# The passage from up to down units in a fast-matrix MLP: split order, who squares the last unit, and where its four sums are made

## The chip, the core and the metric

The kernel runs on one NeuronCore of one Trainium2 chip. Its engines work side by side: TensorE (PE) multiplies into PSUM banks, VectorE (DVE), ScalarE (ACT) and GpSimd (POOL) work elementwise, and SyncE (SP) issues the DMA transfers. Each engine takes its own instructions in the order in which they are written; they meet only at semaphores. The metric is device time in microseconds (us), median of three runs.

## The reference, cut to what matters

A decoder trunk of two layers (a hybrid mixer, then a sparse-attention mixer), 1024 tokens by 1024 channels in fp32. Each layer ends in the same MLP, which is all that the change touches:

```
def squared_relu_mlp(u, w1, w2):
    return jnp.square(jax.nn.relu(u @ w1)) @ w2
...
        h = h + squared_relu_mlp(rms_norm(h, norm_mlp[layer]), mlp_w1[layer], mlp_w2[layer])
```

## The kernel before, in words

Every fp32 operand is split into a high part (rounded by ACT) and a low part (operand minus high part, by DVE or POOL), and each product is three matmuls: high by high, low by high, high by low. One such matmul of 128x512 starts every 0.23 us when PE is not held up.

**The units.** The MLP of each layer runs 14 "up" units (`fast_up`, the hidden columns) and then 14 "down" units (`fast_down`, d = 0 to 13), each a 2x2 block multiplication by Strassen's scheme in Winograd's form: 7 products (i = 0 to 6) of block sums in place of 8, each product 12 matmuls. The weights' sums are made by POOL (`unit_sums`) and split by ACT and DVE (`unit_high`, `unit_low`), unit by unit, ahead of PE.

**The hidden side.** After an up unit, DVE forms the hidden blocks (add a bank of PSUM to a block set aside by ACT in CX, CW, CY, then relu and square) and four sums of them (`hidden_sums`), and SP stores all seven to `hid_d` in HBM (`store_hidden`). The down units take hidden sub-blocks q = 0 to 13 as their other operand, split into high and low by `sub_high` (ACT) and `sub_low` (DVE; POOL for three of q = 1). Down units d and d+1 use the pair q = d and q = d+1 (d even). q = 0 and 1 come straight from SBUF (up units 11 and 12); the others are reloaded from `hid_d` (`load_sub`). The last up unit, 13, is q = 13, used only from d = 12 on. Its blocks are written into `HO[1]` (tiles HOA1, HOB1) over those of unit 11 (q = 0), so each square has to wait until its block of q = 0 is split.

**The passage.** Around the end of up unit 13, DVE runs a list written out by hand: `last_out` (adds that free the PSUM banks), `last_square`, the splits of q = 0 and 1 (`sub_low(q, i)`), those of the weights of unit 14, the first down unit (`unit_low(N_UP, i)`), the first `collect` (adding a down product from PSUM to H) and the four sums of unit 13. `fast_down(0)` on PE waits for its splits by a count in the order in which DVE makes them.

**What SP does then.** In one queue: `load_unit(16)` into the buffer of unit 14's weights, free when unit 14's last splits are done; `store_hidden(13)`; `load_sub(3)`; when the store has landed, the reload of half of the residual H from `hm_d` (it lies where HOA1 and HOB1 were). DVE's `collect(1, 0)`, the first of down unit 1, waits for this reload; PE's product 2 of down unit 1 waits for `collect(1, 0)`, since it goes into the same bank. In the same way product 4 of each down unit waits for `collect(d, 2)`.

Of the kernel before, what the change touches and what calls it, by code (L numbers as in the profile page):

```python
# [85 lines left out]
def build_program(nc, xT, pieces, cst, sel, prm, gatew, relx, onehot, w1c, w2c, blkind, out):  # L86
    ctx = ExitStack()
    with ctx:
# [250 lines left out]
        q_lo = Again(m_rs, 1)  # L339
        q_lop = sem("hidden_lo_pool")  # L340
        s_spill = Again(x_in[1], 16)
        f_back = Again(x_in[2], 16)
# [44 lines left out]
        def sub_raw(q, i):  # L387
# [7 lines left out]
            return (U_rawh, U_raw)[(i - 1) // 3][:, 5 + (i - 1) % 3, T1]  # L395

        def sub_no(L, q, i):

            return 95 * L + 7 * q + i + 1 - 3 * (q > 1)

# [259 lines left out]
        def mlp_pe(pe, first_units, mm3, piece_read, pieces_read_now, sum_squares, spread, p0, layer):  # L660
# [44 lines left out]
            def fast_up(u):  # L705

                gu = N_UP * layer + u
                for i in range(7):
                    b = U_BANKS[u % 2][PROD_BANK[i]]
                    pe.wait_ge(*unit_ready(layer, u, i))  # L710
                    if u == 0 and i in (1, 2, 4, 5):
                        pe.wait_ge(*s_slo.at(4 * layer + (1, 2, 0, 3, 4)[i - 1]))
                    if u == 1 and i == 0:
                        pe.wait_ge(up_free, 8 * layer + 12)
                    if i == 0 and u >= 2:
                        pe.wait_ge(*f_relu.at(gu - 1))
                    elif i == 1 and u >= 2:
                        pe.wait_ge(*f_hid.at(10 * (gu - 2) + 5))
                    elif i == 2:
                        pe.wait_ge(*f_copy.at(3 * gu + 1))  # L720
                    elif i == 3 and u >= 2:
                        pe.wait_ge(*f_hid.at(10 * (gu - 2) + 1))
                    elif i == 4:
                        pe.wait_ge(*f_copy.at(3 * gu + 3))
                    elif i == 6:
                        pe.wait_ge(*f_hid.at(10 * gu + (3 if u < 13 else 2)))
                    for k in range(4):
                        w = slice(k * P, (k + 1) * P)
                        last = mm3(ps[:, b, :], RH[i][:, w], RL[i][:, w], U_SIDE[i][0][:, k, :], U_SIDE[i][1][:, k, :],
                                   k == 0 and i in (0, 1, 3), k == 3, i not in (0, 1, 3))  # L730
                    last.then_inc(f_up.sem, 1)

            def fast_down(d):

                gd, n = N_DOWN * layer + d, N_UP + d
                for i in range(7):
                    pe.wait_ge(*unit_ready(layer, n, i))
                    if d % 2 == 0:
                        pe.wait_ge(*q_lo.at(sub_no(layer, d + 1, min(i, 6 if d else 3))))
                    if d == 0 and i > 3:  # L740
                        pe.wait_ge(*sub_late(layer, i))
                    if d == 0 and i == 0:
                        pe.wait_ge(*f_hid.at(10 * (14 * layer + 13) + 4))
                    if d == 1 and i == 0:
# [36 lines left out]
        def mlp_act(act, layer):  # L781
# [47 lines left out]
            def hidden_last(u):  # L829
# [6 lines left out]
                act.wait_ge(*f_relu.at(gu + 1))  # L836
                A(H21[:], H21[:], ACT.Square).then_inc(sq21.sem, 1)

            def sub_high(q, i):
# [5 lines left out]
                else:  # L845
                    act.wait_ge(*q_in[q % 2].at(16 * (2 + q % 2) * (6 * L + q // 2)))
                act.wait_ge(*sub_free(L, q, i))
                A(sub_tile(q % 3, i)[0], sub_raw(q, i), ACT.Copy).then_inc(q_hi.sem, 1)

# [18 lines left out]
            for u in range(N_UP):  # L868
                for i in range(7):
# [10 lines left out]
                    if u == N_UP - 1 and i >= 3:  # L880
                        if i == 3:
                            sub_high(0, 6)
                        for x in ((0, 1), (2, 3), (4, 5), ())[i - 3]:
                            sub_high(1, x)
            for d in range(N_DOWN - 1):
                for i in range(7):
# [11 lines left out]
        def mlp_dve(dve, sum_first, norm_steps, layer):  # L898
# [43 lines left out]
            def last_out(j):  # L942
# [4 lines left out]
                c = (CX, CW, CY)[j][:]  # L947
                V_.tensor_tensor(c, ps[:, U_BANKS[1][(1, 0, 2)[j]], :], c, ALU.add).then_inc(f_hid.sem, 1)

            def last_square(j):  # L950

                gu = N_UP * L + 13
                c = (CX, CW, CY)[j][:]
                dve.wait_ge(*q_lo.at(sub_no(L, 0, (0, 6, 3)[j])))
                dve.wait_ge(*f_hid.at(10 * gu + (1, 2, 4)[j]))
                V_.scalar_tensor_tensor(HO[1][(0, 6, 3)[j]], c, 0.0, c, ALU.max, ALU.mult).then_inc(f_hid.sem, 1)

            def hidden_sums(u):
# [9 lines left out]
                dve.wait_ge(*f_hid.at(10 * gu + 9))  # L968
                V_.tensor_tensor(t[5], t[3], t[2], ALU.subtract).then_inc(f_hid.sem, 1)

            def sub_low(q, i):
# [78 lines left out]
            last_out(1)  # L1050
            last_square(0)
            sub_low(0, 5)
            last_out(2)
            sub_low(0, 6)
            last_square(1)
            unit_low(N_UP, 3)
            sub_low(1, 0)
            last_square(2)
            for i in range(1, 4):
                sub_low(1, i)  # L1060
            unit_low(N_UP, 4)
            dve.wait_ge(*q_lo.at(sub_no(L, 1, 3)))
            collect(0, 0)
            hidden_sums(N_UP - 1)
            dve.wait_ge(q_lop, 3 * (L + 1))
            for d in range(N_DOWN):
                for i in range(7):
# [6 lines left out]
                    if i and d + 2 < N_DOWN:  # L1074
                        sub_low(d + 2, i - 1)
                    if d == N_DOWN - 1 and i in (4, 5):
                        hidden(0, 2 * (i - 4))
# [80 lines left out]
        def mlp_sp(sp, load, layer):  # L1158
# [33 lines left out]
            def store_hidden(u):  # L1192

                sp.wait_ge(*f_hid.at(10 * (14 * L + u) + 10))
                dma(hid_d[u][:, 0:4, :], HOA[u % 2][:]).then_inc(f_out[u % 2].sem, 16)
# [2550 lines left out]
```

## Time and profile before

| what | value |
|---|---|
| time, median of 3 runs | 2550.36 us (2550.3 to 2551.29) |
| the profiled execution, its own time | 2550.74 us |
| its span, first to last instruction | 2548.8 us |
| PE busy | 2485.8 us (98%) |
| DVE, POOL, ACT busy | 1773.0, 1208.6, 1108.6 us |
| mean granted clock of PE | 0.994 of full speed |

How to read it: the two MLPs are the long dense stretches of PE. The passage of layer 0 lies at about 817 to 857 us of the span, that of layer 1 at 2221 to 2261 us; up to the end of up unit 13, layer 1 repeats layer 0 some 1403.77 us later. Times in the rows below are microseconds from the span's start.

### The profile page before, as it was taken

The page shows a single profiled execution, that of the slowest core. Times are in us where ns is not written, and L with a number is a line of the kernel's source. Part 1 is how long each engine was busy: PE and PEld are TensorE (multiplying, and loading weights), DVE is VectorE, ACT ScalarE, POOL GpSimd, SP SyncE. Part 2 cuts the span into 40 slices and gives each one's busy share as a digit, 9 for nine tenths or more (in the row PEclk, how much of TensorE's full clock was granted, in tenths as well). Part 3 has the DMA queues.
Part 4 walks back from the last instruction along what each step waited for, and adds up shares of the span by engine and source line. Part 5 has one row for each costly group of instructions (what it writes and reads, how often), then busy time and mean ns, then how long its engine had stood idle before and what let it go on. Part 6 is the DMA issues. An engine that isn't in the chain of part 4 may idle for free.

```text
span 2548.8 us, 38266 instructions
## 1 busy us (share of the span) xinstructions
PE 2485.8 (98%) x14136; PEld 2009.7 (79%) x14136; DVE 1773.0 (70%) x2859; ACT 1108.6 (43%) x2142; POOL 1208.6 (47%) x939
## 2 busy tenths in 40 slices
PE   8999999999999999999999999999999999999999
PEld 5778667888887888887877777788788888778887
DVE  6554755476777999973037877676646777899994
ACT  4526644243334344322136666566524333434431
POOL 5462677234445454434215777546523444544441
PEclk9999999999999999999999999999999999999999
DMA  4110003223443544412321112353222344354441
GB/s 173 34 50 34 1 2 116 79 87 138 158 159 108 216 174 143 145 44 122 103 82 57 55 55 76 90 150 88 112 83 87 137 153 165 107 215 155 164 145 66
DMA packets 91711, 275.78 MB, mean 108 GB/s; under 512 B 9879, under 2 KB 39191, under 8 KB 76871
## 3 DMA queue, kind: packets, MB, share of 16 engines
q1 hardware_dynamic: 87976, 255.18, 29.4%
q10 hardware_dynamic: 3552, 18.18, 1.8%
q8 instruction: 114, 1.87, 0.3%
q14 instruction: 69, 0.57, 0.1%
HBM read 197.50 MB, written 73.86 MB: 106 GB/s over the span
## 4 chain that ended last, share of the span: by engine, by line
PE 90%; DVE 3%; issue 2%; POOL 2%; ACT 1%; DMA 1%; DVEq 0%; ACTq 0%; POOLq 0%
PE ps L1738 23%; PE ps L1743 22%; PE ps L1742 22%; PE ps L2305 5%; PE ps L2321 5%; PE ps L2280 2%; PE ps L2295 1%; POOL MX L1537 1%; PE ps L2296 1%; PE ps L1967 1%; PE ps L1996 1%; PE ps L1981 1%; PE ps L2229 1%; PE ps L2121 1%; PE ps L1860 0%
## 5 line engine op out<-in xcount | busy, mean ns | idle before, releaser
L1738 PE MATMUL ps<-U_hi,RH 128*128 128x512 f32 x912 | 356.8, 391 | 10.1 <-issue 10.1
L1742 PE MATMUL ps<-U_lo,RH 128*128 128x512 f32 x912 | 356.7, 391 | 0.0
L1743 PE MATMUL ps<-U_hi,RL 128*128 128x512 f32 x912 | 356.5, 391 | 0.0
L1136 POOL TENSOR_TENSOR RL<-RAW,RH 128x512 fp32r<-128x512 f32 x112 | 152.7, 1363 | 380.6 <-ACT RH L819 380.6
L819 ACT ACTIVATE RH<-RAW 128x512 fp32r<-128x512 f32 x280 | 175.3, 628 | 285.1 <-PE ps L1743 278.9
L1738 PE MATMUL ps<-U_hi,W_hi 128*128 128x512 f32 (+2 forms) x656 | 261.7, 399 | 11.9 <-DVE U_lo L3015 10.5
L1743 PE MATMUL ps<-U_hi,W_lo 128*128 128x512 f32 (+2 forms) x656 | 258.1, 393 | 0.0
L1742 PE MATMUL ps<-U_lo,W_hi 128*128 128x512 f32 (+2 forms) x656 | 258.0, 393 | 0.0
L1738 PE MATMUL ps<-SH,RH 128*128 128x512 f32 x656 | 255.5, 389 | 0.9 <-ACT CX L827 0.9
L1743 PE MATMUL ps<-SH,RL 128*128 128x512 f32 x656 | 255.2, 389 | 0.0
L1742 PE MATMUL ps<-SL,RH 128*128 128x512 f32 x656 | 255.2, 389 | 0.0
L1738 PEld LDWEIGHTS ps<-U_hi,RH 128*128 128x128 f32 x912 | 172.3, 189 | 47.0 <-issue 10.9
L927 DVE TENSOR_TENSOR RL<-RAW,RH 128x512 fp32r<-128x512 f32 x168 | 137.0, 816 | 100.3 <-ACT RH L819 100.3
L1743 PEld LDWEIGHTS ps<-U_hi,RL 128*128 128x128 f32 x912 | 172.3, 189 | 36.2
L1742 PEld LDWEIGHTS ps<-U_lo,RH 128*128 128x128 f32 x912 | 172.2, 189 | 35.7
L1121 POOL TENSOR_TENSOR RT<-RAW 128x512 f32<-128x512 f32 x56 | 77.0, 1375 | 234.2 <-PE ps L1743 160.7
L1454 POOL CAST W_hi<-W_raw 128x2048 fp32r<-128x2048 f32 x28 | 58.8, 2100 | 249.0 <-DMA W_raw<-in_pieces 207.7
L819 ACT ACTIVATE RH<-RT 128x512 fp32r<-128x512 f32 x112 | 70.9, 633 | 213.5 <-POOL RT L1126 111.6
L1738 PEld LDWEIGHTS ps<-U_hi,W_hi 128*128 128x128 f32 (+2 forms) x656 | 122.5, 187 | 44.0 <-DVE U_lo L3015 10.9
L1600 POOL TENSOR_SCALAR PX<-PX,rinv,GATE 128x896 f32<-128x896 f32 (+7 forms) x128 | 104.8, 830 | 99.3 <-DVE rinv L3510 99.1
L3518 DVE COPY PT<-ps 128x512 f32<-128x512 f32 (+1 forms) x192 | 94.3, 519 | 82.2 <-PE ps L2305 82.0
L994 DVE TENSOR_TENSOR H<-H,ps 128x512 f32<-128x512 f32 x212 | 136.2, 677 | 20.5 <-PE ps L1743 18.7
(409 smaller groups left out, 6082.2 us busy)
## 6 DMA issues: line engine op xcount, KB each, us to landing
W_raw<-in_pieces SPq DMA_DIRECT2D x30, 1024.0 KB, 5.1
RAW<-in_pieces SPq DMA_DIRECT2D x28, 1024.0 KB, 5.0
RAW<-in_pieces SPq DMA_DIRECT2D x56, 512.0 KB, 8.2
hid_d<-HOA SPq DMA_DIRECT2D x24, 1024.0 KB, 3.9
hid_d<-HOB SPq DMA_DIRECT2D x24, 768.0 KB, 5.4
RHA<-hid_d SPq DMA_DIRECT2D x12, 1024.0 KB, 5.2
RHB<-hid_d SPq DMA_DIRECT2D x12, 768.0 KB, 7.5
U_rawh<-hid_d SPq DMA_DIRECT2D x12, 768.0 KB, 4.8
```

The costliest lines, as they stand in the source:

```text
L819: A(ring(RH[i], n), src, ACT.Copy).then_inc(u_hi.sem, 1)
L927: V_.tensor_tensor(ring(RL[i], n), src, ring(RH[i], n).bitcast(F32), ALU.subtract).then_inc(u_lod.sem, 1)
L994: V_.tensor_tensor(o, o, ps[:, b[m], :], ALU.add).then_inc(f_ev.sem, 1)
L1121: G_.tensor_tensor(ring(RT[1], n), R[B12], R[B11], ALU.subtract).then_inc(u_add.sem, 1)
L1136: G_.tensor_tensor(ring(RL[i], n), quarter(n, (B22, B11)[i - 5]), ring(RH[i], n).bitcast(F32), ALU.subtract).then_inc(u_lop.sem, 1)
L1600: nc.gpsimd.tensor_scalar(p, p, rinv[:, c:c + 1], GATE[:, i, hd * 3 + 1 + br:hd * 3 + 2 + br], ALU.mult, ALU.mult).then_inc(x_nm, 1)
L1738: m = mm(o, a_hi, b_hi, start=first, stop=False, skip_group_check=again)
L1742: mm(o, a_hi, b_lo, start=False, stop=False, skip_group_check=again)
L1743: return mm(o, a_lo, b_hi, start=False, stop=last, skip_group_check=again)
L2305: m = nc.tensor.transpose(ps[:, b, kb % 4 * P:kb % 4 * P + P], prob(U)[0][:, kb * P:(kb + 1) * P], ident)
L2321: m = mm(ps[DK * e:DK * (e + 1), b, x * P:x * P + P], KV[:, k0 + kb, 1 if br == SEL else 3, hd // HPG, :], PT[(2 * s + e) % 4][:, kb * P:( ...
L3518: V_.tensor_copy(PT[U % 4][:, k0 * P:k1 * P], ps[:, rot("p", U, j), 0:(k1 - k0) * P]).then_inc(x_cpv, 1)
```

## The change

- DVE splits q = 0 and q = 1 in the order in which PE's first down unit uses them (`Q_FIRST` gives the place of each in the count), and makes the first `collect` earlier.
- The last unit's relu and square go from DVE (one instruction for each of three blocks) to ACT (a relu and a square for each), after the last weights' split of unit 14. A semaphore of their own (`last_unit_banks_read`) now tells PE that the banks are free. The fourth block's square is written straight into `HO[1][1]`.
- The four sums of unit 13 are not made in the passage. `store_hidden(13)` goes out when the squares are done; the sums are made when q = 13 is back in SBUF, by DVE in down unit 11 (`late_sum`), and ACT's `sub_high(13, i)` of those four blocks waits for them.

```diff
+        Q_FIRST = ((0, 0), (0, 1), (0, 2), (0, 3), (0, 4), (1, 0), (1, 1), (1, 2), (0, 6), (1, 3), (0, 5))
...
                     if d % 2 == 0:
-                        pe.wait_ge(*q_lo.at(sub_no(layer, d + 1, min(i, 6 if d else 3))))
+                        pe.wait_ge(*q_lo.at(sub_no(layer, d + 1, i) if d else
+                                            max(sub_no(layer, 0, i), sub_no(layer, 1, min(i, 3)))))
...
                     if d == 0 and i == 0:
-                        pe.wait_ge(*f_hid.at(10 * (14 * layer + 13) + 4))
+                        pe.wait_ge(last_read, 3 * layer + 3)
...
+            def last_square(n, j):
+                gu = N_UP * L + 13
+                c = (CX, CW, CY)[j][:]
+                act.wait_ge(last_read, 3 * L + j + 1)
+                A(c, c, ACT.Relu).then_inc(f_hid.sem, 1)
+                act.wait_ge(*f_hid.at(10 * gu + 2 * n + 1))
+                act.wait_ge(*q_lo.at(sub_no(L, 0, (0, 6, 3)[j])))
+                A(HO[1][(0, 6, 3)[j]], c, ACT.Square).then_inc(f_hid.sem, 1)
...
+            def late_sum(j):
+                g0 = 10 * (14 * L + 13) + 6
+                r = [sub_raw(13, i) for i in range(7)]
+                if j:
+                    dve.wait_ge(*f_hid.at(g0 + j))
+                else:
+                    dve.wait_ge(*q_in[1].at(48 * (6 * L + 6)))
+                o, x, y, op = ((r[4], r[0], r[1], ALU.subtract), (r[1], r[1], r[6], ALU.add),
+                               (r[2], r[1], r[0], ALU.subtract), (r[5], r[3], r[2], ALU.subtract))[j]
+                V_.tensor_tensor(o, x, y, op).then_inc(f_hid.sem, 1)
...
             last_out(1)
-            last_square(0)
+            sub_low(1, 0)
+            sub_low(1, 1)
+            last_out(2)
+            sub_low(1, 2)
+            sub_low(0, 6)
+            unit_low(N_UP, 3)
+            dve.wait_ge(*q_lo.at(sub_no(L, 1, 2)))
+            collect(0, 0)
+            sub_low(1, 3)
             sub_low(0, 5)
-            last_out(2)
-            sub_low(0, 6)
-            last_square(1)
-            unit_low(N_UP, 3)
-            sub_low(1, 0)
-            last_square(2)
-            for i in range(1, 4):
-                sub_low(1, i)
             unit_low(N_UP, 4)
-            dve.wait_ge(*q_lo.at(sub_no(L, 1, 3)))
-            collect(0, 0)
-            hidden_sums(N_UP - 1)
+            dve.wait_ge(*q_lo.at(95 * L + 11))
...
+                    if d == 11 and i < 3:
+                        for j in ((0, 1), (2,), (3,))[i]:
+                            late_sum(j)
...
             def store_hidden(u):
-                sp.wait_ge(*f_hid.at(10 * (14 * L + u) + 10))
+                if u == N_UP - 1:
+                    sp.wait_ge(*f_hid.at(10 * (14 * L + u) + 6))
+                    sp.wait_ge(*sq21.at(14 * L + u + 1))
+                else:
+                    sp.wait_ge(*f_hid.at(10 * (14 * L + u) + 10))
```

The order of the built programs shows the moves. First DVE in the passage of layer 0, before, from the second `last_out` (CW) to the last split of unit 14's weights (RL4). HOA0 and HOB0 hold q = 1, HOA1 and HOB1 hold q = 0 and then unit 13; `SCALAR_TENSOR_TENSOR` is a `last_square`; U_lo, SL0 and SL1 are the low parts of hidden blocks.

```order
L948 TENSOR_TENSOR CW_130<-ps,CW_130 128x512
L956 SCALAR_TENSOR_TENSOR HOA1_126<-CX_129 128x512
L975 TENSOR_TENSOR SL1_123<-HOB1_128,SH1_120 128x512
L948 TENSOR_TENSOR CY_131<-ps,CY_131 128x512
L975 TENSOR_TENSOR U_lo_88<-HOB1_128,U_hi_87 128x512
L956 SCALAR_TENSOR_TENSOR HOB1_128<-CW_130 128x512
L927 TENSOR_TENSOR RL3_104<-RAW0_115,RH3_97 128x512
L975 TENSOR_TENSOR U_lo_88<-HOA0_125,U_hi_87 128x512
L956 SCALAR_TENSOR_TENSOR HOA1_126<-CY_131 128x512
L975 TENSOR_TENSOR U_lo_88<-HOA0_125,U_hi_87 128x512
L975 TENSOR_TENSOR SL0_122<-HOA0_125,SH0_119 128x512 x2
L927 TENSOR_TENSOR RL4_105<-RAW0_115,RH4_98 128x512
```

The same place with the change:

```order
L972 TENSOR_TENSOR CW_130<-ps,CW_130 128x512
L1003 TENSOR_TENSOR U_lo_88<-HOA0_125,U_hi_87 128x512 x2
L972 TENSOR_TENSOR CY_131<-ps,CY_131 128x512
L1003 TENSOR_TENSOR SL0_122<-HOA0_125,SH0_119 128x512
L1003 TENSOR_TENSOR U_lo_88<-HOB1_128,U_hi_87 128x512
L951 TENSOR_TENSOR RL3_104<-RAW0_115,RH3_97 128x512
L1020 COPY H_70<-ps 128x512 x2
L1003 TENSOR_TENSOR SL0_122<-HOA0_125,SH0_119 128x512
L1003 TENSOR_TENSOR SL1_123<-HOB1_128,SH1_120 128x512
L951 TENSOR_TENSOR RL4_105<-RAW0_115,RH4_98 128x512
L1020 COPY H_70<-ps 128x512 x2
```

The first split of q = 1 (`U_lo<-HOA0`), eighth in the first list, is now second, right behind `last_out` of CW; the three squares are gone; two copies of `collect(0, 0)` stand ahead of the last three splits instead of behind them; the four sums that came behind the copies before are gone too.

Second, DVE at the start of down unit 11 in layer 0, with the change. `U_raw`, `U_rawh` and `RHC` hold q = 13 as reloaded; lines L997 are the four late sums, L1022 and L1033 are `collect`, and the second pair of L1022 with the third is `collect(11, 1)` and `collect(11, 2)`.

```order
L1022 TENSOR_TENSOR H_70<-H_70,ps 128x512 x2
L997 TENSOR_TENSOR U_raw_150<-RHC_149,U_rawh_151 128x512
L997 TENSOR_TENSOR U_rawh_151<-U_rawh_151,U_raw_150 128x512
L1022 TENSOR_TENSOR H_70<-H_70,ps 128x512 x2
L951 TENSOR_TENSOR RL0_101<-RAW0_115,RH0_94 128x512
L1003 TENSOR_TENSOR U_lo_88<-RHC_149,U_hi_87 128x512
L997 TENSOR_TENSOR U_rawh_151<-U_rawh_151,RHC_149 128x512
L1022 TENSOR_TENSOR H_70<-H_70,ps 128x512 x2
L951 TENSOR_TENSOR RL1_102<-RT1_109,RH1_95 128x512
L1003 TENSOR_TENSOR U_lo_88<-U_rawh_151,U_hi_87 128x512
L997 TENSOR_TENSOR U_raw_150<-U_rawh_151 128x512
```

Without the four lines L997 this is the list of before; three of them stand ahead of `collect(11, 2)`.

Third, ACT at the end of the passage, with the change, from the square of the fourth block to the first weights' split of down unit 1 (RH0 from RAW1):

```order
L847 ACTIVATE HOA1_126<-H21_132 128x512
L827 ACTIVATE RH6_100<-RAW0_115 128x512
L854 ACTIVATE CX_129<-CX_129 128x512
L857 ACTIVATE HOA1_126<-CX_129 128x512
L854 ACTIVATE CY_131<-CY_131 128x512
L857 ACTIVATE HOA1_126<-CY_131 128x512
L854 ACTIVATE CW_130<-CW_130 128x512
L857 ACTIVATE HOB1_128<-CW_130 128x512
L827 ACTIVATE RH0_94<-RAW1_116 128x512
```

The six instructions L854 and L857 are new; before, RH0 followed RH6.

## Rows read from the trace of the kernel before

**Rows 1.** PE's waits: engine, line, awaited: us in total, times, longest.
```profile
PE ps L1738 <- issue: 10.1, 2, 5.1
...
PE ps L1996 <- DVE MIX L3266: 4.7, 4, 2.7
...
PE ps L1738 <- DVE U_lo L2912: 2.3, 1, 2.3
```

**Rows 2.** Timeline of PE, layer 0: start, us, line, instruction [idle before].
```profile
828.35 0.54 PE L1738 MATMUL ps<-U_hi,RH 128*128 128x512 f32 x1 [5.05 <-issue]
...
832.07 0.39 PE L1738 MATMUL ps<-U_hi,RH 128*128 128x512 f32 x1
...
854.56 0.39 PE L1738 MATMUL ps<-SH,RH 128*128 128x512 f32 x1
```

**Rows 3.** Timeline of PE, layer 1.
```profile
2232.12 0.77 PE L1738 MATMUL ps<-U_hi,RH 128*128 128x512 f32 x1 [5.05 <-issue]
...
2238.50 0.40 PE L1738 MATMUL ps<-U_hi,RH 128*128 128x512 f32 x1
...
2259.68 0.47 PE L1738 MATMUL ps<-SH,RH 128*128 128x512 f32 x1
```

**Rows 4.** Timeline of DVE in the passage, layer 0.
```profile
826.51 1.75 DVE L975 TENSOR_TENSOR U_lo<-HOA,U_hi 128x512 fp32r<-128x512 f32 x1
...
831.66 0.68 DVE L927 TENSOR_TENSOR RL<-RAW,RH 128x512 fp32r<-128x512 f32 x1
```

**Rows 5.** Timeline of POOL in the passage, layer 0.
```profile
821.39 1.30 POOL L1136 TENSOR_TENSOR RL<-RAW,RH 128x512 fp32r<-128x512 f32 x1 [4.60 <-ACT RH L819]
...
835.80 1.52 POOL L1121 TENSOR_TENSOR RT<-RAW 128x512 f32<-128x512 f32 x1 [6.42 <-PE ps L1743]
```

**Rows 6.** Timeline of ACT, layer 0: the first weights' split of down unit 1.
```profile
833.02 0.63 ACT L819 ACTIVATE RH<-RAW 128x512 fp32r<-128x512 f32 x1 [7.91 <-PE ps L1743]
```

**Rows 7.** Timeline of SP's DMA queue, layers 0 and 1.
```profile
832.37 1.23 SPq L1185 DMA_DIRECT2D RAW<-in_pieces  x2
836.21 0.33 SPq L1195 DMA_DIRECT2D hid_d<-HOA  x1
...
842.93 0.81 SPq L1249 DMA_DIRECT2D H<-hm_d  x2
...
2236.14 1.23 SPq L1185 DMA_DIRECT2D RAW<-in_pieces  x2
2240.87 0.33 SPq L1195 DMA_DIRECT2D hid_d<-HOA  x1
```

**Rows 8.** H reload, layer 0: time from issue to landing of its two transfers.
```profile
DMA to landing us min/median/max: 7.2/8.2/9.3
```

**Rows 9.** Timeline of DVE: `collect(1, 0)` in layer 0 and in layer 1.
```profile
852.64 1.28 DVE L994 TENSOR_TENSOR H<-H,ps 128x512 f32<-128x512 f32 x2
...
2258.84 1.28 DVE L994 TENSOR_TENSOR H<-H,ps 128x512 f32<-128x512 f32 x2 [1.21 <-DMA H<-hm_d]
```

**Rows 10.** Stretches: length, busy (instructions) of five engines, clock, DMA share, GB/s.
```profile
834.00:842.00 8.00, 8.00 (x37) 6.64 (x36) 7.96 (x12) 2.46 (x6) 5.96 (x4) 1.00 1.02 352
...
842.50:852.50 10.00, 10.00 (x45) 8.23 (x44) 10.00 (x14) 4.43 (x9) 3.16 (x3) 1.00 1.03 412
...
2240.60:2241.90 1.30, 1.30 (x7) 1.08 (x6) 1.30 (x3) 0.00 (x0) 0.75 (x1) 1.00 0.56 199
```

**Rows 11.** The same columns: PE's clock after two of its waits.
```profile
1170.00:1173.20 3.20, 3.20 (x8) 2.53 (x9) 3.13 (x5) 1.26 (x2) 0.00 (x0) 0.50 0.00 0
294.40:297.60 3.20, 2.64 (x25) 1.95 (x26) 1.92 (x8) 0.88 (x4) 1.82 (x2) 1.00 0.00 0
```

**Rows 12.** Timeline of DVE and PE in down unit 11, layer 0.
```profile
1045.16 0.69 DVE L994 TENSOR_TENSOR H<-H,ps 128x512 f32<-128x512 f32 x1 [0.43 <-PE ps L1743]
...
1048.73 1.27 DVE L994 TENSOR_TENSOR H<-H,ps 128x512 f32<-128x512 f32 x2
...
1050.40 0.39 PE L1738 MATMUL ps<-SH,RH 128*128 128x512 f32 x1
```

More of the change, by code:

```diff
@@ L340, in build_program @@
         q_lop = sem("hidden_lo_pool")
+        last_read = sem("last_unit_banks_read")
         s_spill = Again(x_in[1], 16)
@@ L395, in sub_raw @@
             return (U_rawh, U_raw)[(i - 1) // 3][:, 5 + (i - 1) % 3, T1]
+        Q_FIRST = ((0, 0), (0, 1), (0, 2), (0, 3), (0, 4), (1, 0), (1, 1), (1, 2), (0, 6), (1, 3), (0, 5))
         def sub_no(L, q, i):
+            if q < 2:
+                return 95 * L + Q_FIRST.index((q, i)) + 1
             return 95 * L + 7 * q + i + 1 - 3 * (q > 1)
@@ L724, in fast_up @@
                         pe.wait_ge(*f_copy.at(3 * gu + 3))
+                    elif i == 6 and u < 13:
+                        pe.wait_ge(*f_hid.at(10 * gu + 3))
                     elif i == 6:
-                        pe.wait_ge(*f_hid.at(10 * gu + (3 if u < 13 else 2)))
+                        pe.wait_ge(last_read, 3 * layer + 2)
                     for k in range(4):
@@ L836, in hidden_last @@
                 act.wait_ge(*f_relu.at(gu + 1))
-                A(H21[:], H21[:], ACT.Square).then_inc(sq21.sem, 1)
+                if u == N_UP - 1:
+                    act.wait_ge(*q_lo.at(sub_no(L, 0, 1)))
+                A(HO[1][1] if u == N_UP - 1 else H21[:], H21[:], ACT.Square).then_inc(sq21.sem, 1)
+            def last_square(n, j):
[6 more added lines that the diff above has]
+                A(HO[1][(0, 6, 3)[j]], c, ACT.Square).then_inc(f_hid.sem, 1)
             def sub_high(q, i):
@@ L847, in sub_high @@
                 act.wait_ge(*sub_free(L, q, i))
+                if q == 13 and i in (1, 2, 4, 5):
+                    act.wait_ge(*f_hid.at(10 * (14 * L + 13) + {1: 8, 2: 9, 4: 7, 5: 10}[i]))
                 A(sub_tile(q % 3, i)[0], sub_raw(q, i), ACT.Copy).then_inc(q_hi.sem, 1)
@@ L884, in mlp_act @@
                             sub_high(1, x)
+            for n, j in enumerate((0, 2, 1)):
+                last_square(n, j)
             for d in range(N_DOWN - 1):
@@ L947, in last_out @@
                 c = (CX, CW, CY)[j][:]
[L948 to L956, printed above, removed]
+                V_.tensor_tensor(c, ps[:, U_BANKS[1][(1, 0, 2)[j]], :], c, ALU.add).then_inc(last_read, 1)
             def hidden_sums(u):
@@ L1192, in store_hidden @@
             def store_hidden(u):
-                sp.wait_ge(*f_hid.at(10 * (14 * L + u) + 10))
+                if u == N_UP - 1:
+                    sp.wait_ge(*f_hid.at(10 * (14 * L + u) + 6))
+                    sp.wait_ge(*sq21.at(14 * L + u + 1))
+                else:
+                    sp.wait_ge(*f_hid.at(10 * (14 * L + u) + 10))
                 dma(hid_d[u][:, 0:4, :], HOA[u % 2][:]).then_inc(f_out[u % 2].sem, 16)
```

## The prediction

> **What bounds the kernel now.** I read PE's waits first. PE hardly waits, and of the few stalls two are of one kind: twice, 5.05 us, on L1738 [rows 1]. The view names no releaser ("issue"), so I took PE's timeline: the stall lies between the last matmul of up unit 13 and the first of down unit 0, in both layers [rows 2, 3]. In the code, PE's count of splits for product 0 includes the first split of q = 1, which DVE makes last but three; in layer 0 that is the instruction of 826.51, which ends at 828.26, just before PE starts. The passage is therefore bound by DVE, and DVE by GpSimd: where a split meets a POOL instruction it takes 1.75 us, where it does not, 0.68 [rows 4], and POOL's own takes 1.30 [rows 5].
>
> The stall costs more than its length. The matmul before it ended at 828.35 - 5.05 = 823.30; matmuls last 0.39 and follow each other at 0.23, so the next could have started at 823.14. After the stall, nine starts take 832.07 - 828.35 = 3.72 us, PE being at the lower of its two clock levels; 99 more bring product 2 of down unit 1 at 854.56, 0.227 each [rows 2]. Without stall and slow clock that product, 108 matmuls in, would start at 823.14 + 24.53 = 847.7: **6.9 us** lost. In layer 1 the same points are 2226.91 and 2251.4, against 2259.68, with fifteen slow starts in 6.38 us [rows 3]: **8.2 us** lost. So 15.1 us, 0.59% of the time, is all that the passage can give.
>
> Then I asked what is late next, so SP's queue and the DMA stretches. DVE's first `collect` of down unit 1 waits for the reload of H. In layer 0 the second reload transfer lands 9.3 us after its issue at about 843.3 [rows 7, 8], at 852.6, and DVE starts at 852.64; in layer 1 DVE sits idle 1.21 us for it, until 2258.84, and PE's product 2 comes at 2259.68, just behind [rows 9, 3]. This reload is already as late as PE can bear.
>
> **The change part by part.**
>
> *The new order of splits.* Until the second `last_out` nothing moves. The two splits that PE now needs follow it without POOL in the way and end near 820.9, the third `last_out` near 821.5: both ahead of 823.14. Product 0 starts without a stall, and the clock has no reason to fall: 6.9 and 8.2 us are won here, if nothing takes them back. For product 2 PE needs `collect(0, 0)` by 828.6. DVE makes three instructions that meet POOL (3 x 1.7 from 821.5), then the two copies (from PSUM; such copies are not slowed), done at 827.8. That fits.
>
> *Squares on ACT.* Six instructions of 0.6 us, 3.6 us. They fall into ACT's idle time of 7.91 us before 833.02 [rows 6]; ACT reaches the next weights' split at about 828.7 instead of 826, and DVE comes to that operand only near 833. Price nothing; with the cover gone, at most 2.7 us.
>
> *DVE after the copies.* PE is now ahead, so POOL's sums for the next unit start at 829, when product 1 ends, and not at 835.8 [rows 5]. The last three splits meet them. Without POOL they would end at 829.6, all three behind a POOL instruction at 832.9; I take 831.8, since one POOL instruction is left of the old unit and one or two of the new fall in. Before it was 832.3 [rows 4]. So `load_unit(16)` is issued only 0.5 us earlier, at 831.9. Next come two copies, a split, and a split of q = 2 behind POOL: `collect(0, 2)` has its first copy at 835.8. PE wants it for product 4 at 834.05: a **new wait of 1.9 us**. It is not an extra term, since a later wait swallows it.
>
> *The H reload.* The store of unit 13 now follows `load_unit(16)` by 1.25 us instead of 3.8 and 4.7 us [rows 7]. But that load, the store, `load_sub(3)` and H go through one set of DMA engines, busy all the while: share 1.02 and 1.03 on both sides of 842.25 [rows 10]. If only bytes count, H lands earlier by the 0.5 us of the load, at 852.1; in layer 1 also by the free 0.44 of 1.3 us [rows 10], 0.6, at 2257.7. That is one bound. The other: the 2.9 MB of load and store, 352 GB/s, would move at the 412 of the stretch behind them, 7.0 us in place of 8.2; with the 0.5, H lands at 850.9 and, with the gap, at 2256.5. I take the middle, 851.5 and 2257.1. The copy takes 0.68 and PE follows within 0.15, so product 2 of down unit 1 starts at 852.35 and 2257.95. Gain: **2.2 and 1.7 us** of the 15.1 (bounds 2.7 to 5.1 together).
>
> *The clock.* PE would reach that product at 847.7 + 1.9 = 849.6, and waits 2.8 us; in layer 1 at 2253.3, and waits 4.6. After 2.3 us (L2912) the clock is at the low level for all of the next 3.2 us; after 2.7 us, at another place (MIX), it is not [rows 1, 11]. I take a fall, since matmuls of this form follow here as behind the first of these, and the smaller of the two prices seen, 3.72 - 9 x 0.227 = 1.7 us; in layer 1 before, it was 6.38 - 15 x 0.227 = 3.0. Cost: **1.7 per layer**, 3.4 (0 to 6.0).
>
> *The late sums.* Four DVE instructions of at least 0.60 each move from the passage, where they held up the store alone, into down unit 11. There DVE is booked out: one pause of 0.43 us at the start of the unit [rows 12]. Three of the four stand ahead of `collect(11, 2)`, whose first copy ends at 1049.4; PE takes it at 1050.40, a margin of 0.9 with the semaphore. Least price: 4 x 0.60 - 0.43 = 2.0 us of lateness, of which the margin may hide 0.9, or all, if no later collect is tight. Highest: each of the three behind a POOL instruction, 3 x 1.75 - 0.9 = 4.4. I take **2.0 per layer**: 1.1 at product 4, the rest when the backlog of the fourth reaches the next unit. Total 4.0 (0 to 8.8).
>
> The Trainium skill's page "SBUF — State Buffer", section "Who interferes with whom", says that a VectorE instruction with two SBUF inputs and a GpSimd one that reads SBUF take a shared port in turn, and the loser is blocked for the whole of the other; one with at most one SBUF input does not contend. The rows agree on which ones meet; on the price they show 1.75 - 0.68 = 1.1 us for a loser, where the page's whole instruction would be the 1.30 of POOL's row. By the page the highest price would be 3 x (0.60 + 1.30) - 0.9 = 4.8 us per layer instead of 4.4. It speaks against the move: the sums have two SBUF inputs.
>
> *Sum.* -3.9 + 3.4 + 4.0 = +3.5 us. The profiled execution took 2550.74 us, 1.94 of them outside its span; with the change 2554.2. The median of the runs is 0.38 below that execution, so **2553.9 us**: +0.14%. A measurement of this kernel tells 0.2%, 5.1 us, from no change.
>
> **The rivals.**
> 1. *The main case*: passage won, given back at the H reload, by the clock and in unit 11. 2551 to 2557. Chance 0.45.
> 2. *The sums are hidden, or the clock stays up.* For it: PE waits nowhere in the down units before, and one 2.7 us wait left the clock alone. -3.9 with one of the two prices gone gives +0.1 or -0.5, with both gone 2546.5. From 2546 to 2551. Chance 0.17.
> 3. *The reload is not the limit.* If transfers queued close together move faster than these stretches show, and H lands before PE arrives (849.6 less 0.8, so by 848.8, 16.9 us after the load's issue where it was 20.2), the 15.1 us are won less the new waits at product 4 (2 x 1.9) and the sums (4.0): -7.3, 2543. Against it: the full DMA share. Chance 0.10.
> 4. *Slower beyond measurement*: the waits in unit 11 reach 2 us, so the clock falls there too (1.7 per layer), and in layer 1 it stays low as long as before (3.0 instead of 1.7): 3.5 + 3.4 + 1.3 = +8.2, 2558.6. It decides at a wait of some 2 us ahead of product 4: two of the three sums behind a POOL instruction. Chance 0.28.
>
> **How the numbers follow.** The prediction is the likeliest case. Faster by over 0.2% is rival 3 alone, 0.10. Slower by over 0.2% is rival 4, and 0.02 from the upper end of the main case: 0.30. The same: the rest, 0.60. The range leaves out rival 3 and the far end of rival 4, about 0.18: 2546 to 2559.
>
> **What would show it.** Right: no PE wait at the start of down unit 0; one of 1 to 2 us ahead of product 4 of down unit 0; one of 2 to 5 us ahead of product 2 of down unit 1, released by L1022 behind a DMA wait on H; 0.50 clock behind it; `load_unit(16)` within 0.7 us of before, though its store comes 2.6 us earlier; waits of about 1 us in down units 11 and 12. Wrong: H landing before 850, which makes it faster; no waits in units 11 and 12, which takes 4 us off; a wait at product 0 or 2 of down unit 0, which would mean that the order of splits did not remove the stall.

## The result, and the profile after

| what | before | after |
|---|---|---|
| time, median | 2551.47 us (2550.3 to 2553.48, 9 runs) | 2557.74 us (2552.76 to 2563.42, 9 runs) |
| ratio to before, with its interval | | 1.0021 (1.0012 to 1.003) |
| the profiled execution, its own time | 2550.74 us | 2557.03 us |
| its span; mean clock of PE | 2548.8 us; 0.994 | 2555.2 us; 0.992 |

The change makes the kernel 0.21% slower, 5.4 us by the ratio. The stall ahead of down unit 0 [rows 1] is gone; two other waits have come in the passage, and a short one in down unit 11. PE's timeline in the profile after, layer 0 and then layer 1; the bracket is the idle time before the instruction and what ended it:

```profile
825.35 0.39 PE L1771 MATMUL ps<-U_hi,RH 128*128 128x512 f32 x1
...
838.29 0.47 PE L1771 MATMUL ps<-SH,RH 128*128 128x512 f32 x1 [1.90 <-DVE H L1020]
...
856.91 0.77 PE L1771 MATMUL ps<-SH,RH 128*128 128x512 f32 x1 [4.73 <-DVE H L1022]
...
861.28 0.40 PE L1775 MATMUL ps<-SL,RH 128*128 128x512 f32 x1
...
1055.88 0.47 PE L1771 MATMUL ps<-SH,RH 128*128 128x512 f32 x1 [0.85 <-DVE H L1022]
...
2231.38 0.39 PE L1771 MATMUL ps<-U_hi,RH 128*128 128x512 f32 x1
...
2262.83 0.76 PE L1771 MATMUL ps<-SH,RH 128*128 128x512 f32 x1 [4.62 <-DVE H L1022]
...
2267.59 0.40 PE L1776 MATMUL ps<-SH,RL 128*128 128x512 f32 x1
```

825.35 and 2231.38 are product 0 of down unit 0, without a wait. The kernel before could have started it at 823.14 and 2226.91, so the after trace runs 2.21 us late into the passage of layer 0 and 4.47 into that of layer 1. I take these off when I compare: the 4.47 holds what layer 0 lost, but most of the 2.21 arose in the first 60 us, which the change does not touch.

The other rows are the ends of three waits: product 4 of down unit 0 (838.29), product 2 of down unit 1 (856.91, 2262.83), product 4 of down unit 11 (1055.88). Product 2 of down unit 1 comes at 856.91 - 2.21 = 854.70, against 854.56 before [rows 2]: in layer 0 nothing is left of the passage's gain. In layer 1 it comes at 2258.36, against 2259.68 [rows 3]: 1.3 us are left. Behind it the clock is low until 861.28 and 2267.59.

SP's queue of the profile after, layer 0, answers to [rows 7]:

```profile
834.09 1.23 SPq L1214 DMA_DIRECT2D RAW<-in_pieces  x2
835.42 0.56 SPq L1228 DMA_DIRECT2D hid_d<-HOA  x1
...
844.88 0.81 SPq L1282 DMA_DIRECT2D H<-hm_d  x2
```

The store follows the load by 1.33 us, where it was 3.84. Yet the reload behind it is issued at 844.88 - 2.21 = 842.67, against 842.93. DVE's `collect(1, 0)`, to [rows 9], shows when it landed:

```profile
856.08 2.48 DVE L1022 TENSOR_TENSOR H<-H,ps 128x512 f32<-128x512 f32 x4 [6.09 <-DMA H<-hm_d]
...
2261.99 2.48 DVE L1022 TENSOR_TENSOR H<-H,ps 128x512 f32<-128x512 f32 x4 [5.98 <-DMA H<-hm_d]
```

On before's time that is 853.87 and 2257.52. Before, the reload landed near 852.6 and at 2258.84: in layer 0 it is 1.2 us later, not earlier, though it is issued a little sooner. From issue to landing its two transfers take (to [rows 8]):

```profile
DMA to landing us min/median/max: 8.6/9.7/10.8
```

The DMA's stretches come next (length, busy and instructions of five engines, clock, DMA share, GB/s; to [rows 10]). The changed kernel:

```profile
835.50:839.00 3.50, 1.60 (x7) 1.04 (x7) 3.50 (x5) 1.97 (x4) 3.10 (x2) 1.00 0.90 259
...
845.00:852.00 7.00, 7.00 (x32) 5.62 (x30) 4.99 (x6) 2.52 (x5) 2.42 (x2) 1.00 1.05 415
...
834.09:854.09 20.00, 16.18 (x71) 12.75 (x69) 15.90 (x21) 7.89 (x15) 8.71 (x7) 1.00 0.93 354
```

and before:

```profile
834.00:835.80 1.80, 1.80 (x10) 1.49 (x9) 1.76 (x4) 0.17 (x1) 0.00 (x0) 1.00 0.96 312
...
841.00:842.50 1.50, 1.50 (x8) 1.25 (x7) 1.50 (x2) 1.50 (x4) 1.50 (x1) 1.00 0.86 210
...
832.37:852.37 20.00, 20.00 (x90) 16.48 (x89) 19.94 (x27) 8.24 (x15) 9.62 (x6) 1.00 0.94 350
```

While `load_unit(16)` and the store run side by side, the DMA engines are busy (0.90) and move 259 GB/s, against 415 behind. The Trainium skill's "HBM Reference", section "Specifications (TRN2)", says that a core streaming alone measures about 425 GB/s: the stretch behind agrees, the one of load and store does not. But this is not what makes the reload late. The kernel before has slow stretches too, 312 GB/s while the load runs alone and 210 near the store's end, and over the 20 us from the load's issue the engines move no fewer bytes with the change (354 GB/s) than before (350).

What is late is the reload's tail, its last packets. The reload moves 256 packets of 8 KB. By the trace's records of single packets the 240th starts 19.1 us after the load's issue in layer 0 of both kernels, the last one at 19.5 us before and at 21.2 with the change. In layer 1 before has such a tail as well (20.2 and 21.9 us; 19.2 and 21.1 with the change). Of these four places only layer 0 of before was spared it. Why the tail is long in one place and short in another, no run here shows.

### The profile page after: what moved, and what is told of

It is laid out like the page before. It is cut to its first block, busy times and chain, and to the rows that moved or that the text cites. A ratio compares the mean times of both kernels' runs of the same rounds, so it can differ in the third digit from the quotient of the medians.

```text
span 2555.2 us, 38274 instructions
## 1 busy us (share of the span) xinstructions
PE 2487.1 (97%) x14136; PEld 2009.3 (79%) x14136; DVE 1766.3 (69%) x2853; ACT 1115.7 (44%) x2154; POOL 1206.4 (47%) x939
## 4 chain that ended last, share of the span: by engine, by line
PE 86%; DVE 6%; issue 2%; DMA 2%; POOL 2%; ACT 1%; SPq 0%; DVEq 0%; ACTq 0%; POOLq 0%
PE ps L1771 21%; PE ps L1776 21%; PE ps L1775 21%; PE ps L2338 5%; PE ps L2354 5%; PE ps L2313 2%; PE ps L2328 1%; PE ps L2329 1%; POOL MX L1570 1%; PE ps L2000 1%; PE ps L2029 1%; PE ps L2014 1%; DVE SL L1003 1%; DMA H<-hm_d 1%; DMA hid_d<-HOB 1%
## 5 line engine op out<-in xcount | busy, mean ns | idle before, releaser
L1022 DVE TENSOR_TENSOR H<-H,ps 128x512 f32<-128x512 f32 x212 | 136.3, 677 | 33.4 <-PE ps L1776 20.6
L1771 PEld LDWEIGHTS ps<-SH,RH 128*128 128x128 f32 x656 | 124.2, 189 | 44.5 <-issue 18.9
```

What stands on the lines that cost most here:

```text
L1022: V_.tensor_tensor(o, o, ps[:, b[m], :], ALU.add).then_inc(f_ev.sem, 1)
L1771: m = mm(o, a_hi, b_hi, start=first, stop=False, skip_group_check=again)
```

## The experiments

All were timed against the kernel before on the same chip, so ratios are compared, not medians. A ratio's interval is about 0.1% either way, 2.5 us; the traces decide between neighbours. Waits are those of layer 0.

| run | median us | ratio (interval) | PE's waits: unit 0 / unit 1 / units 11 and 12 |
|---|---|---|---|
| changed kernel | 2557.74 | 1.0021 (1.0012 to 1.003) | 1.90 / 4.73 / 0.85 |
| e1, reload ahead of load_sub(3) | 2551.78 | 0.9998 (0.9989 to 1.0006) | 1.90 / 2.94 / 0.85 |
| e2, store ahead of load_unit(16) | 2545.56 | 0.9973 (0.9964 to 0.9981) | 1.91 / 0 / 0.84 |
| e3, both | 2546.22 | 0.9973 (0.9963 to 0.9983) | 1.91 / 0 / 0.84 |
| b1, e1's move in the kernel before | 2552.92 | 1.0 (0.9991 to 1.0008) | 5.06 (ahead of it) / 0 / 0 |
| e4, evictions first in unit 0 | 2556.72 | 1.0017 (1.0008 to 1.0026) | 1.29 / 5.24 / 0.85 |
| e5, e3 and splits behind the evictions | 2542.83 | 0.9958 (0.9945 to 0.9971) | 0 / 0 / 0.85 |
| e6, sums back in the passage | 2556.66 | 1.0013 (1.0005 to 1.0022) | 5.66 / 0 / 0 |
| e9, e6 with squares on DVE | 2558.41 | 1.0018 (1.0009 to 1.0027) | 7.78 / 0 / 0 |
| e7, e3 with sums one step later | 2548.29 | 0.9977 (0.9968 to 0.9987) | 1.91 / 0 / 0.74, 0.58 |
| e10, e5 with sums on POOL | 2543.26 | 0.9958 (0.9944 to 0.9971) | 0 / 0 / 0.87, 0.61 |
| e11, e5 without the sums | 2536.87 | 0.9935 (0.9921 to 0.9948) | 0 / 0 / 0 |
| e12, e5 with sums in the passage | 2552.21 | 1.0 (0.999 to 1.0011) | 4.46 / 0 / 0 |

### Is the reload the limit, and what makes it late?

My theory: the passage's gain is lost to the reload, which queues behind other transfers. Rival: squares and late sums cost the time. e1:

```diff
             store_hidden(13)
-            load_sub(3)
             sp.wait_ge(*stored(L, 13))
             for c in (2, 6):
                 dma(H[:, c:c + 2, :], hm_d[:, c:c + 2, :]).then_inc(f_back.sem, 16)
+            load_sub(3)
             load_residual(0)
```

> The reload of H is issued ahead of the three transfers of load_sub(3); nothing else changes. Theory (the end of the passage is set by the landing of the reload, which queues behind load_unit(16), the store and load_sub(3) in the same DMA engines): without the 1.75 MB of load_sub(3) beside it the store lands 1 to 2 us earlier and the reload is alone behind it, so that H lands near 851 us in layer 0 instead of 856.1; TensorE's wait before product 2 of down unit 1 falls from 4.7 us to between 0 and 1.5 in each layer, with part of the low clock behind it, and the kernel takes 7 to 12 us less than the changed kernel (2546 to 2551 us). Rival (the squares on ScalarE and the four late sums are what costs; the reload only takes up time that would be lost anyway): within 1 us of the changed kernel, 2557 us.

e2:

```diff
-            load_unit(N_UP + 2)
             store_hidden(13)
+            load_unit(N_UP + 2)
             load_sub(3)
```

> The store of unit 13 is issued ahead of load_unit(16); nothing else changes. Theory: the squares are done 3 us before the store is issued now (830.8 against 835.4 us in layer 0), so the store starts near 832 us with the DMA engines free, lands by 840 and not at 844.9; the reload is then issued some 4 us earlier, but stands behind load_unit(16) and load_sub(3), so that H lands 2 to 4 us earlier and the wait before product 2 of down unit 1 falls from 4.7 to between 1 and 3 us: 4 to 8 us less than the changed kernel, 2550 to 2554 us. Rival (the reload is not the limit, or the same bytes end at the same time in whatever order they are issued): no change, 2557 us, with the wait still at 4.7.

e3 has both edits.

> Both moves of the two runs before: store ahead of load_unit(16), reload ahead of load_sub(3). Theory: the store is issued near 832 us in layer 0 and lands near 839; the reload behind it has only load_unit(16) beside it and lands by 848 us, before VectorE asks for it at 850. The wait before product 2 of down unit 1 is gone in both layers (4.7 and 4.6 us) and so is the low clock behind it (2 us each): 12 to 14 us less than the changed kernel, 2543 to 2546 us. Rival (all of these bytes must pass before down unit 1 in any case, so that load_unit(16) or load_sub(3) becomes what is late): a wait of 3 us or more before units 1 to 3 of the down half instead, 2552 us or more.

b1 is e1's edit in the kernel before.

> The kernel before, with the reload of H issued ahead of the three transfers of load_sub(3); nothing of the change. Theory (before the change the stall stood ahead of down unit 0, and the reload came almost in time): VectorE waits 1.2 us for the reload in each layer and TensorE shows no wait there, so 0 to 2 us less than the kernel before, 2549.5 to 2551.5 us; the gain of 6 us that the same move gives the changed kernel belongs to the change's own stall. Rival (the order of these transfers costs the same 3 us per layer whatever stands ahead of it): 2545 us.

The rival falls: moving transfers alone takes 0.23% (e1) and 0.48% (e2, e3) off the changed kernel, which is then level with the kernel before or faster. But e1 gave a little less than I had said, waits of 2.94 us in layer 0 and of 1.99 in layer 1 stayed, each with a low clock behind it, and it did not work as I had thought. The store was to land sooner without `load_sub(3)` beside it; the landing times (KB of one, us from issue) in e1 and in e2 say otherwise. First e1:

```profile
hid_d<-HOA SPq DMA_DIRECT2D x1, 1024.0 KB, 8.1
...
hid_d<-HOB SPq DMA_DIRECT2D x1, 768.0 KB, 9.8
```

and e2:

```profile
hid_d<-HOA SPq DMA_DIRECT2D x1, 1024.0 KB, 3.9
...
hid_d<-HOB SPq DMA_DIRECT2D x1, 768.0 KB, 5.9
```

It is the load just ahead of it that slows the store (8.1 and 9.8 us; in the changed kernel 7.7 and 8.8), not what follows it: in e2 the same follows, and it takes 3.9 and 5.9. Part of this is waiting in turn: at the 312 GB/s that it moves alone, the load's 1.05 MB take 3.4 us, and the store is issued 1.3 us behind it, which gives an estimate of 2.1 of the 3.8 us by which its first part lands later than in e2 (7.7 and 3.9). The rest would be the lower rate of the two side by side, the 259 GB/s above; no run separates it. e1 gains because the reload then stands alone. e2 shows that SP's order of store and load holds the reload back: with the store first it is issued, on before's time, at 838.65 - 3.29 = 835.36 in place of 842.67; VectorE finds H there, and the wait is gone. Moving the reload too (e3) adds nothing that can be measured. SP's queue of e3:

```profile
830.56 0.32 SPq L1228 DMA_DIRECT2D hid_d<-HOA  x1
...
833.75 1.67 SPq L1214 DMA_DIRECT2D RAW<-in_pieces  x2
836.78 0.80 SPq L1281 DMA_DIRECT2D H<-hm_d  x2
```

and `collect(1, 0)` in e3, without a wait:

```profile
849.54 1.87 DVE L1022 TENSOR_TENSOR H<-H,ps 128x512 f32<-128x512 f32 x3
```

In the kernel before the same move is worth nothing (b1), as expected: there the stall of 5.06 us stands ahead of down unit 0, and PE never waited for H.

### Is the wait at product 4 a cost of its own?

e4:

```diff
-                    if d or i:
+                    if (d or i) and (d or i != 2):
                         collect(d, i)
+                    if d == 0 and i == 1:
+                        collect(0, 2)
```

> On VectorE collect(0,2) is moved ahead of the splits unit_low(15,0) and sub_low(2,0), so that the banks of product 4 of down unit 0 come free 2.4 us earlier; nothing else changes. Theory (that wait is swallowed by the later one for the reload): the 1.9 us wait before product 4 of down unit 0 goes in both layers with its low clock, and the wait before product 2 of down unit 1 grows by as much, from 4.7 to about 8.5 us; the time stays within 1.5 us of the changed kernel. Rival (each wait costs by itself): 3.8 us less per layer, 2550 us.

Not while the reload is late: the time moves by 0.04%. The wait at product 4 goes, a smaller one comes at product 6, and the reload's grows, by 0.5 us only and not by 4. The two waits together hardly change (6.63 us, then 6.53): their end is the landing of the reload. In e5, on top of e3 and of this edit, the splits of q = 2 in down unit 0 move behind the evictions (each `collect`, which empties a bank of PSUM) as well:

```diff
-                    if i and d + 2 < N_DOWN:
+                    if d == 0 and i > 3:
+                        for x in ((0,), (1, 2), (3, 4, 5))[i - 4]:
+                            sub_low(2, x)
+                    elif d and i and d + 2 < N_DOWN:
                         sub_low(d + 2, i - 1)
```

> On top of the run with store and reload both ahead: in down unit 0 VectorE evicts first (collect(0,2) directly behind collect(0,1)) and makes the splits sub_low(2,0) to (2,6), which only down unit 2 needs, behind collect(0,4), collect(0,5) and collect(0,6) instead of one after each collect. Theory (with the reload out of the way the 1.9 us wait before product 4 of down unit 0 and the low clock behind it are no longer swallowed): both go in both layers without a new wait, 1.9 + 2.0 us each, so 7 to 8 us less than the run with both ahead, 2538 to 2540 us. Rival (VectorE has no slack in down units 0 and 1, the work only comes later): a wait of 1 us or more before product 6 of unit 0 or in unit 1 or 2, 2543 us or more.

Half of it came: 0.15%, 3.8 us, and no wait is left in either passage. The other half was my mistake: I had put 2.0 us of low clock behind this wait too. PE's clock in the changed kernel (length, busy, clock, DMA share, GB/s) is full behind 838.29 and halved behind 856.91:

```profile
838.20:840.00 1.80, 1.71 (x8) 1.00 0.99 337
...
856.80:858.00 1.20, 1.09 (x3) 0.50 0.98 410
```

### What the late sums and the squares are worth

e6 puts the sums back, in place on `HO[1]`:

```diff
+            passage_sums()
             dve.wait_ge(q_lop, 3 * (L + 1))
...
-                    if d == 11 and i < 3:
-                        for j in ((0, 1), (2,), (3,))[i]:
-                            late_sum(j)
...
-                if u == N_UP - 1:
-                    sp.wait_ge(*f_hid.at(10 * (14 * L + u) + 6))
-                    sp.wait_ge(*sq21.at(14 * L + u + 1))
-                else:
-                    sp.wait_ge(*f_hid.at(10 * (14 * L + u) + 10))
+                sp.wait_ge(*f_hid.at(10 * (14 * L + u) + 10))
```

> The changed kernel with the four sums of unit 13 back in the passage (on VectorE behind unit_low(14,4), ahead of collect(0,1)), the store waiting for them, and none at the reload. Theory (the earlier store bought nothing, since it shared the DMA engines with load_unit(16)): the store is issued 2 to 4 us later and lands about as before, the reload of H lands within 1 us of 856.1; the wait before product 4 of down unit 0 grows from 1.9 to 4 to 5 us and the one for the reload shrinks by as much; only the 0.85 us waits in down unit 11 and their low clock go, 1.0 to 1.2 us per layer: 2554 to 2557 us. Rival (the late sums are what makes the store and with it the reload early): the reload lands 2 us or more later, 2560 us or more.

SP's queue of e6:

```profile
835.57 1.23 SPq L1208 DMA_DIRECT2D RAW<-in_pieces  x2
840.41 0.33 SPq L1218 DMA_DIRECT2D hid_d<-HOA  x1
...
847.17 0.81 SPq L1272 DMA_DIRECT2D H<-hm_d  x2
```

The store goes out 4.84 us behind the load, and the reload follows 6.8 us later; in the changed kernel it was 1.33 and 9.5. So the 3.5 us by which the late sums bring the store forward move the reload 0.8 us nearer to the load in layer 0; in layer 1 it comes 12.2 us behind the load, against 11.7 in e6. The wait for the evictions grew to 5.66 us, the one for the reload went, the time did not change beyond its interval.

e9 then takes the squares back to DVE, in front of the sums, which leaves the new order of splits alone:

```diff
+            for n, j in enumerate((0, 2, 1)):
+                last_square(n, j)
             passage_sums()
```

> The new order of splits alone: the changed kernel with the three squares back on VectorE (behind unit_low(14,4)) and the four sums behind them in the passage, the store waiting for both, no sums at the reload. Theory (the order removes the stall ahead of down unit 0 whatever becomes of the squares; what VectorE still has to do then stands ahead of the evictions for product 4): product 0 starts without a wait, and the wait before product 4, 5.7 us with the squares on ScalarE, grows by three squares of 0.7 to 1.8 us to 8 to 9.5 us; the store and the reload come 2 to 4 us later; 4 to 8 us more than with the sums alone put back, 2560 to 2565 us. Rival (the squares were never on the path, so ScalarE's help is worth nothing): 2555 to 2558 us.

Product 0 starts without a wait, so the order alone, with the squares behind the splits, removes the stall. The wait at product 4 grows by 2.1 us to 7.78, and the time by 0.05%, both less than I had said. The three squares last 4.2 us, but two of them now meet POOL instead of two of the sums, which shrink. DVE in e9, a square beside POOL, the last one, and a sum:

```profile
836.99 1.76 DVE L979 SCALAR_TENSOR_TENSOR HOA<-CY 128x512 f32<-128x512 f32 x1
838.68 0.68 DVE L979 SCALAR_TENSOR_TENSOR HOB<-CW 128x512 f32<-128x512 f32 x1
839.46 0.69 DVE L989 TENSOR_TENSOR HOB<-HOA 128x512 f32<-128x512 f32 x1
```

The sums' own price was tried in three ways. e7, on e3:

```diff
-                    if d == 11 and i < 3:
-                        for j in ((0, 1), (2,), (3,))[i]:
+                    if d == 11 and i < 4:
+                        for j in ((0, 1), (), (2,), (3,))[i]:
```

> On top of the run with store and reload both ahead: the third and the fourth late sum of down unit 11 are made one step later each, behind collect(11,2) and collect(11,3), so that none stands on VectorE between collect(11,1) and collect(11,2). Theory (the late sums cost time only where one of them, 1.77 us beside GpSimd, delays the eviction for product 4): the 0.84 us wait before product 4 of down unit 11 goes in both layers and no other takes its place, 1.5 to 2.5 us less than the run with both ahead, 2543.5 to 2545 us. Rival (VectorE has no slack in unit 11, so that 3 to 4 us of sums cost about 1 us wherever they stand): a wait before product 5 or 6 or in unit 12 instead, no change.

The rival was right. PE in e7:

```profile
1052.36 0.47 PE L1771 MATMUL ps<-U_hi,RH 128*128 128x512 f32 x1 [0.74 <-DVE H L1022]
...
1061.39 0.47 PE L1771 MATMUL ps<-SH,RH 128*128 128x512 f32 x1 [0.58 <-DVE H L1022]
```

The wait at product 4 goes, and two others come, 1.3 us in place of 0.84. e10, on e5:

```diff
             for n in range(N_W):
+                if n == N_UP + 12:
+                    for j in range(4):
+                        late_sum(j)
                 unit_sums(n)
```

> On top of the fastest run so far (store and reload ahead, splits of sub_low(2) behind the evictions): the four late sums on GpSimd, ahead of its sums for unit 26, where it is idle 3.5 us now. Theory (VectorE has no slack in down unit 11, GpSimd has): the 0.85 us wait before product 4 of down unit 11 goes in both layers, 1.5 to 2.4 us less, 2540.5 to 2541.5 us. Rival (GpSimd's sums slow VectorE's splits beside them, 0.68 to 1.78 us each, by as much as they take from it): a wait of 0.5 us or more stays in unit 11 or 12, no change.

The rival again: 0.87 and 0.61 us of waits. DVE's splits meet more of POOL's work, and DVE waits once for a weights' split that POOL's sums of weights, now behind the late sums, have made late:

```profile
1047.84 1.23 DVE L951 TENSOR_TENSOR RL<-RT,RH 128x512 fp32r<-128x512 f32 x1 [0.66 <-ACT RH L827]
1048.99 1.77 DVE L991 TENSOR_TENSOR U_lo<-U_rawh,U_hi 128x512 fp32r<-128x512 f32 x1
...
1052.64 0.69 DVE L991 TENSOR_TENSOR SL<-U_rawh,SH 128x512 fp32r<-128x512 f32 x1
```

e11 leaves the four calls of `late_sum`, and the waits for them, out of e5:

```diff
-                    if d == 11 and i < 3:
-                        for j in ((0, 1), (2,), (3,))[i]:
-                            late_sum(j)
```

> On top of the fastest run so far, the four late sums left out (the last unit's four combined squares are then missing from the output). It measures what they cost on VectorE in down unit 11. Theory (0.85 us of wait in each layer, and nothing further on): 1.5 to 2.4 us less than that run, 2540.5 to 2541.5 us, with no wait in units 11 and 12. Rival (the 2.0 us per layer of the prediction, with part of it not seen as a wait): 4 us less, 2538.8 us.

No wait is left in units 11 and 12. Matmul by matmul (each trace holds the same 14136), e11 starts 0.37 us behind e5 just before product 4 of down unit 11 in layer 0 and 0.76 ahead ten matmuls later: the late sums' price on the path is 1.1 us per layer (in layer 1 also), 2.2 in all. The changed kernel set against before in the same way shows it too: 4.47 us behind ahead of this product and 5.58 after it, 5.35 and 6.44 in layer 1. By this measure the sums cost 1.9 us per layer in e7 and 2.0 in e10; that e10 is as fast as e5 hides it. The time is 6.0 us shorter. The other 3.8 come in stretches that no edit touches. PE in e5, between the MLPs (length, busy, clock, DMA share, GB/s):

```profile
1115.00:1130.00 15.00, 14.02 (x63) 0.89 0.01 2
...
1615.00:1626.00 11.00, 9.34 (x50) 0.84 1.02 238
```

and in e11:

```profile
1115.00:1130.00 15.00, 14.02 (x70) 1.00 0.01 2
...
1615.00:1626.00 11.00, 9.44 (x69) 1.00 0.84 196
```

The clock is full there in e11 and not in e5. It is full there in e10 too, which makes the sums, so the sums do not decide it; why it falls is open.

e12 is e6's edit on e5.

> The fastest whole kernel so far (store and reload ahead, splits of sub_low(2) behind the evictions) with the four sums back in the passage, ahead of collect(0,1), and none at the reload. It asks what the late sums are worth where the reload no longer hides it. Theory (VectorE has no idle time in the passage, so 3 to 5 us of sums delay the eviction for product 4 and the store): a wait of 2.5 to 4.5 us before product 4 of down unit 0, and the store some 5 us later; 0.85 us come back in down unit 11; 1.7 to 5.5 us more per layer, 2546 to 2553 us. Rival (without the low clock and the reload's wait the passage has room for the sums): 2541 to 2543 us.

PE in e12:

```profile
842.78 0.77 PE L1766 MATMUL ps<-SH,RH 128*128 128x512 f32 x1 [4.46 <-DVE H L1016]
```

All of e5's gain is gone (1.0 against 0.9958): with the reload out of the way, 2.2 us in unit 11 of both layers together buy back a wait of 4.5 us and its low clock in each layer. The third part of the change is worth 0.42% there, which the changed kernel could not show. What the squares on ACT are worth on e5 was not tried.

## Why the prediction was right in its direction, and where it was not

The time lies in the range and 3.8 us above the forecast; the forecast was no measurable change, the result stands at the edge of what can be told from it (0.21%). It is beyond the main case's 2557 and near the 2558.6 of rival 4, but not by that rival's path: the wait in unit 11 is 0.85 us, and the clock stays full behind it. Point by point:

- **The new order of splits** and **the squares on ACT**: as said. Product 0 starts at once in both layers, and e9 shows that the order does it. RH0, forecast for about 828.7, came at 830.79 - 2.21 = 828.6.
- **The new wait at product 4**: 1.9 forecast, 1.90 and 1.91 measured, and swallowed by the later one (e4).
- **The H reload: this step failed, in layer 0.** The load was issued when I said (831.9). From there I let the bytes move at 352 or at 412 GB/s, and between these bounds took 851.5 for the landing; it was 853.87, outside both. The rate was no lower than before: 354 GB/s over the 20 us from the load's issue, against 350. What I had wrong is that bytes and rate give the landing. I counted from layer 0 of before, where the reload ends without a tail; with the change its last packets come 1.7 us later after the load's issue than there. The term of 2.2 us became -0.1. In layer 1 the reload landed at 2257.52 (2257.1 forecast, bound 2257.7): 1.3 in place of 1.7. That the order of transfers keeps the reload late enough to stop PE is shown by e2: with the store first, the wait is gone. Why the tail varies stays open.
- **The clock**: it falls behind the reload's wait and only there. 861.28 - 856.91 less ten starts of 0.227 is 2.1 us, in layer 1 2.3; I had taken the smaller price seen, 1.7. That it would fall I had said for a wait of 2.8 us in layer 0; behind waits of 2.68 us the runs show both levels (last section), so it might have gone either way, and the wait became 4.73.
- **The late sums**: 2.0 per layer forecast, 1.1 measured (e11, and the changed kernel against before). The 1.1 at product 4 was in the forecast; the backlog that was to cost 0.9 more in the next unit did not.

By these terms: 0.1 - 1.3 + 4.4 + 2.2 = +5.4 us, which is what the ratio gives; I had -3.9 + 3.4 + 4.0 = +3.5. Errors partly cancel: 2.7 us too much hope in the reload and 1.0 in the clock, 1.8 too much fear of the sums. The two profiled executions differ by 6.3 us; the other 0.9 lie outside these places and are less than single runs differ.

## What to carry to other kernels

Before you bring a transfer forward, look at what waits for its landing, and do not take bytes over a rate for that landing: the same bytes in the same time ended 1.7 us apart here. Before you put a late landing down to a low rate in one stretch, count the bytes over the whole way in both traces. If a cure removes a stall and the time does not fall, look for the next thing that was just in time, and judge the cure's parts again once that is out of the way: here the same three edits give +0.2%, or -0.4% with two transfers and one loop of DVE in another order. On an engine that is booked out, moving work a step later moves the wait with it; here it made it dearer, 1.9 us in place of 1.1.

## What the runs showed of the hardware that I had not expected

- A 1 MB load (in two transfers) and a 1.75 MB store issued within 1.3 us of each other moved 259 GB/s at a DMA share of 0.90 (layer 0 of the changed kernel), against 415 for reads behind them; the load alone moved 312 (before). The load's packets are 1 KB in the trace, those of the reads behind it 2 and 8 KB; whether this or the two directions is the cause was not tried. The store's parts took 7.7 and 8.8 us to land, 3.9 and 5.9 when the store was issued 3 us ahead.
- PE kept its full clock behind waits of 1.90 and 1.91 us, and went to the low level behind one of 1.99 (e1, layer 1), one of 2.94 (e1, layer 0) and all the longer ones of these passages; behind those of 4.73 and 4.62 us this cost 2.1 and 2.3 us. The length of a wait alone does not decide: far from any edit, every trace has the same wait for DVE's MIX, 2.68 or 2.69 us, between 294 and 298 us, and the clock stays full behind it in the kernel before [rows 11] and in the changed one, and falls to 0.50 in e6, e10 and e11.
- Sums moved from DVE to POOL gave DVE nothing (e10): its splits beside POOL last 1.77 us in place of 0.69, and POOL's sums took 1.30 to 1.74. The Trainium skill's "SBUF — State Buffer", section "Who interferes with whom", has it that the one of the two that issues first keeps the other out; the rows agree that they hold each other up, but do not show which issued first.
- Runs of one kernel spread over 8 us (2548.46 to 2556.91 for the kernel before, in one set), and the clock in stretches far from any edit (0.84 or 1.00) moved the time by up to 4 us, more than most terms of this study.
